# Router's end reordered on VectorE, between the router and the first expert item of a hybrid decoder trunk

## The reference

```python
def moe_swiglu(h, w_router, w1, w3, w2):
    logits = jnp.dot(xf.astype(F32), w_router.astype(F32))
    top_logit, top_e = lax.top_k(logits, TOP_K)          # 2 of 8 experts for each token
    gates = jax.nn.softmax(top_logit, axis=-1)
    ...
    padded = (counts + ROW_BLOCK - 1) // ROW_BLOCK * ROW_BLOCK
    dest = pstart[e_sorted] + (jnp.arange(n * TOP_K, dtype=jnp.int32) - start[e_sorted])
    ...
    x_rows = jnp.concatenate([xf, jnp.zeros((1, d), xf.dtype)], axis=0)[row_tok]
    def expert_block(args):
        xb, e = args
        return (jax.nn.silu(xb @ w1[e]) * (xb @ w3[e])) @ w2[e]   # 1024 -> 3584 -> 1024
    ...
    y = jax.ops.segment_sum(y_rows.astype(F32) * row_gate[:, None], row_tok, num_segments=n + 1)[:n]
```

## Time and profile before

| | before |
|---|---|
| median of 3 executions | 2046.12 us (2045.82 to 2048.55) |
| the profiled execution, whole | 2042.14 us |
| its span | 2040.5 us |
| busy PE, DVE, ACT, POOL | 98%, 77%, 54%, 6% |
| chain that ended last, by engine | PE 86%, DVE 9%, issue 2%, ACT 2% |

### The profile page before, as it was taken

How to read it: one execution, slowest core, us unless ns; L and a number is a source line. 1 busy time by engine, 2 the same in 40 slices (tenths; PEclk the granted TensorE clock), 3 DMA queues, 4 the chain that set the end, 5 groups by cost and what they waited for, 6 DMA issues and landing times.

```text
span 2040.5 us, 34437 instructions
## 1 busy us (share of the span) xinstructions
PE 1990.0 (98%) x12290; PEld 1761.5 (86%) x12291; DVE 1570.0 (77%) x1978; ACT 1101.6 (54%) x1273; POOL 116.5 (6%) x104
## 2 busy tenths in 40 slices
PE   7999999999999999999999999999999999999997
PEld 6889787878779788999999988888999888999875
DVE  6866535353557585888888899999888898888998
ACT  6532423232335423555655577777655777555775
POOL 0000000000000000300100010100100100000250
PEclk9999999999999999999999999999999999999999
DMA  5312723232322123877787799999877899877993
GB/s 198 105 61 93 269 82 103 82 103 82 106 79 83 62 73 131 247 267 260 240 279 247 248 343 379 352 390 362 282 264 258 290 384 353 280 255 247 332 410 130
DMA packets 218751, 449.50 MB, mean 220 GB/s; under 512 B 13264, under 2 KB 64480, under 8 KB 218704
## 3 DMA queue, kind: packets, MB, share of 16 engines
q1 hardware_dynamic: 210560, 421.05, 59.1%
q0 software_dynamic: 8144, 27.82, 3.6%
HBM read 431.87 MB, written 16.96 MB: 220 GB/s over the span
## 4 chain that ended last, share of the span: by engine, by line
PE 86%; DVE 9%; issue 2%; ACT 2%; DMA 0%; DVEq 0%; ACTq 0%; SPq 0%; POOLq 0%
PE ps L617 17%; PE ps L619 17%; PE ps L618 17%; PE ps L959 15%; PE ps L976 8%; PE ps L961 6%; PE ps L978 3%; DVE w_lo L1845 1%; PE ps L686 1%; DVE w_lo L1848 1%; DVE w_lo L1401 1%; PE ps L641 1%; DVE ex L1426 1%; ACT w_hi L1251 0%; PE ps L880 0%
## 5 line engine op out<-in xcount | busy, mean ns | idle before, releaser
L959 PE MATMUL ps<-xt,w_hi 128*128 128x304 f32 x1792 | 457.2, 345 | 2.9 <-issue 2.9
L1845 DVE TENSOR_TENSOR w_lo<-raw,w_hi 128x1024 fp32r<-128x1024 f32 x336 | 409.3, 1218 | 55.3 <-ACT w_hi L1251 52.2
L1251 ACT ACTIVATE w_hi<-raw 128x1024 fp32r<-128x1024 f32 x340 | 357.7, 1052 | 123.5 <-PE ps L961 73.3
L961 PE MATMUL ps<-xt,w_lo 128*128 128x152 f32 x1792 | 420.0, 234 | 0.0
L1848 DVE TENSOR_TENSOR w_lo<-raw,w_hi 128x1024 fp32r<-128x1024 f32 x336 | 408.8, 1217 | 0.0
L1253 ACT ACTIVATE w_hi<-raw 128x1024 fp32r<-128x1024 f32 x340 | 356.5, 1049 | 1.1 <-DMA raw<-in_moe_w_dram 1.1
L961 PEld LDWEIGHTS ps<-xt,w_lo 128*128 128x128 f32 x1792 | 342.9, 191 | 0.1
L959 PEld LDWEIGHTS ps<-xt,w_hi 128*128 128x128 f32 x1792 | 338.8, 189 | 3.5 <-issue 3.4
L617 PE MATMUL ps<-act_hi,w_hi 128*128 128x512 f32 x608 | 242.1, 398 | 5.2 <-DVE act_lo L1446 5.2
L619 PE MATMUL ps<-act_hi,w_lo 128*128 128x512 f32 x608 | 239.9, 395 | 0.0
L618 PE MATMUL ps<-act_lo,w_hi 128*128 128x512 f32 x608 | 239.8, 394 | 0.0
(11 more groups left out here) (362 smaller groups left out, 3222.6 us busy)
## 6 DMA issues: line engine op xcount, KB each, us to landing
raw<-in_moe_w_dram SPq DMA_DIRECT2D x672, 512.0 KB, 5.4
raw<-in_w_in_dram SPq DMA_DIRECT2D x19, 1024.0 KB, 5.1
raw<-in_ffn_w_gate_dram SPq DMA_DIRECT2D x11, 1024.0 KB, 5.3
raw<-in_ffn_w_up_dram SPq DMA_DIRECT2D x11, 1024.0 KB, 5.3
raw<-in_ffn_w_down_dram SPq DMA_DIRECT2D x11, 1024.0 KB, 4.9
raw<-in_w_out_dram SPq DMA_DIRECT2D x8, 1024.0 KB, 4.9
y_rows<-mult POOLq DMA_DIRECT2D x1, 8192.0 KB, 28.9
y_rows<-yacc POOLq DMA_DIRECT2D x7, 512.0 KB, 5.2
```

What stands on the lines that cost most here:

```text
L959: pe.matmul(pairs_of(ps[:, bank, 0:2 * NW]), hi_[:, k % 4, f * P:(f + 1) * P], xt[:, k, :, 0:NW], start=k == 0, stop=False)
L961: last = pe.matmul(ps[:, bank, NW:2 * NW], lo_[:, k % 4, f * P:(f + 1) * P], xt[:, k, 0, 0:NW], start=False, stop=k == KT - 1)
L1251: act.activation(slot_hi[p % 6][:, 0:half], raw6(p)[:, 0:half], ACT.Copy).then_inc(w_hi_half, 1)
L1845: dve.tensor_tensor(slot_lo[p % 6][:, 0:half], raw6(p)[:, 0:half], f32(slot_hi[p % 6][:, 0:half]), ALU.subtract)
```

## The change

On DVE, the low part of piece 0 is split: its first half stays ahead of the ranks, its second half moves behind the first part of the item list. The semaphore `pick_ready` is raised for each token tile, and PE waits for tile i before its first matmul that uses it. The item list is made in two parts: the number of items, the last item and the flags for the turned form come early (`items_ready` 1), the expert and block of each item late (`items_ready` 2). Between the two lie now the rest of piece 0, piece 1, the low parts of the picked rows, and pieces 2 and 3. The computation of `slots` comes behind these. SP and POOL wait for 2, PE and ACT still for 1. PE's fillings are 6 and 6 in place of 13 and 14.

```diff
             expert(0, 0, True)
-            sp.wait_ge(items_ready, 1)
+            sp.wait_ge(items_ready, 2)
...
-            pool.wait_ge(items_ready, 1)
+            pool.wait_ge(items_ready, 2)
...
-            spin(ps[:, 7, 0:P], 13)
-            pe.wait_ge(pick_ready, 1)
+            spin(ps[:, 7, 0:P], 6)
             for k in range(KT):
                 for i in range(NT):
+                    if k == 0:
+                        pe.wait_ge(pick_ready, i + 1)
                     last = pe.matmul(ps[:, k // 3, k % 3 * NW:(k % 3 + 1) * NW], rows_of(3, i)[:, k * P:(k + 1) * P],
                                      pick[:, i, :], start=i == 0, stop=i == NT - 1)
...
-            spin(ps[:, 7, 0:P], 14)
+            spin(ps[:, 7, 0:P], 6)
             turned_next = pe.alloc_register("pe_turned_next")
             pe.wait_ge(items_ready, 1)
...
+            def rest_half(p, at_, late):
+                half = PIECE // 2
+                s_ = slice(late * half, (late + 1) * half)
+                if late:
+                    dve.wait_ge(w_hi_done, MOE0 + p + 1 if at_ is None else at_ + (MOE0 + p + 1))
+                else:
+                    dve.wait_ge(w_hi_half, p + 1 if at_ is None else at_ + (p + 1))
+                ins = dve.tensor_tensor(slot_lo[p % 6][:, s_], raw6(p)[:, s_], f32(slot_hi[p % 6][:, s_]), ALU.subtract)
+                if late:
+                    ins.then_inc(w_lo_done, 1)
...
-            rest_ahead(0, None)
+            rest_half(0, None, 0)
             dve.wait_ge(rank_done, 1)
...
+            link(dve.tensor_copy(items[0:1, 48:64], flags))
+            link(dve.tensor_copy(items[0:1, 32:33], items_to[:, NE - 1:NE]))
+            dve.tensor_copy(items[0:1, 33:34], last_item[:, NE - 1:NE]).then_inc(items_ready, 1)
+            dve.wait_ge(items_ready, 1)
+
+            rest_half(0, None, 1)
+            rest_ahead(1, None)
+            picked_rows(0)
+            picked_rows(1)
+            rest_ahead(2, None)
+            rest_ahead(3, None)
...
             dve.tensor_copy(items[0:1, 0:32], rt[0:1, 18, :]).then_inc(items_ready, 1)
-            dve.wait_ge(items_ready, 1)
-            picked_rows(0)
-            picked_rows(1)
-            rest_ahead(2, None)
-            rest_ahead(3, None)
             dve.wait_ge(par_act, DEPTH + 1)
```

More of the change, by code:

```diff
@@ L1840, in _ @@
             slot_lo = [w_los[:, (MOE0 + j) % 3, :] for j in range(3)] + [w_lo2[:, j, :] for j in range(3)]
-            def rest_ahead(p, at_):
[L1843 to L1849, removed]
+            def rest_half(p, at_, late):
[8 more added lines that the diff above has]
+                    ins.then_inc(w_lo_done, 1)
+            def rest_ahead(p, at_):
+                for late in range(2):
+                    rest_half(p, at_, late)
             def picked_rows(j):
@@ L1869, in _ @@
             for i in range(NT):
-                ins = dve.tensor_scalar(pick[:, i, :], mcon[:, MC_ROW:MC_ROW + NW], rt[:, RK, i * NE:i * NE + 1],
-                                        rt[:, CH, i * NE:i * NE + 1], ALU.is_equal, ALU.mult)
-            ins.then_inc(pick_ready, 1)
+                dve.tensor_scalar(pick[:, i, :], mcon[:, MC_ROW:MC_ROW + NW], rt[:, RK, i * NE:i * NE + 1],
+                                  rt[:, CH, i * NE:i * NE + 1], ALU.is_equal, ALU.mult).then_inc(pick_ready, 1)
             link(dve.tensor_reduce(cnt, ps[:, 4, 0:NT * NE].rearrange("p (t e) -> p e t", e=NE), AX.X, ALU.add))
@@ L1877, in _ @@
             link(dve.tensor_tensor(first_block, blocks_to, blocks, ALU.subtract))
[L1879 to L1886, removed]
             w3v = [rtw[0:1, i, :].rearrange("p (n e) -> p n e", e=NE) for i in range(5)]
@@ L1902, in _ @@
             link(dve.tensor_tensor_scan(items_to, items_e, zero_row[0:1], 0.0, ALU.add, ALU.add))
+            link(dve.tensor_scalar(last_item, items_to, -1.0, None, ALU.add))
+            link(dve.tensor_tensor(w3v[3], n_row, over_n(last_item), ALU.is_equal))
+            link(dve.tensor_tensor(w3v[3], w3v[3], over_n(turned_e), ALU.mult))
+            link(dve.tensor_reduce(flags, w3v[3], AX.X, ALU.add))
+            link(dve.tensor_copy(items[0:1, 48:64], flags))
[8 more added lines that the diff above has]
+            rest_ahead(3, None)
+            link(dve.tensor_scalar(rt[:, 15, 0:8], first_block, float(P), None, ALU.mult))
+            link(dve.tensor_tensor(r3(SLOT), r3(RK), per_e(rt[:, 15, 0:8]), ALU.add))
+            for j, oh in enumerate((OH1, OH2)):
+                link(dve.tensor_tensor(r3(PROD), r3(SLOT), r3(oh), ALU.mult))
+                link(dve.tensor_reduce(rt[:, 16, 4 * j:4 * j + 4], r3(PROD), AX.X, ALU.add))
+                link(dve.tensor_copy(slots[:, :, j], rt[:, 16, 4 * j:4 * j + 4]))
+            dve.tensor_copy(tokens[:, :], mcon[:, MC_TOK:MC_TOK + NT]).then_inc(slots_ready, 1)
             link(dve.tensor_tensor(first_item, items_to, items_e, ALU.subtract))
             link(dve.tensor_tensor(shift, first_block[0:1], first_item, ALU.subtract))
-            link(dve.tensor_scalar(last_item, items_to, -1.0, None, ALU.add))
             link(dve.tensor_tensor(w3v[0], n_row, over_n(first_item), ALU.is_ge))
@@ L1913, in _ @@
             link(dve.tensor_tensor(rt[0:1, 18, 16:32], rt[0:1, 18, 16:32], n_row[:, :, 0], ALU.add))
-            link(dve.tensor_tensor(w3v[3], n_row, over_n(last_item), ALU.is_equal))
-            link(dve.tensor_tensor(w3v[3], w3v[3], over_n(turned_e), ALU.mult))
-            link(dve.tensor_reduce(flags, w3v[3], AX.X, ALU.add))
             link(dve.tensor_scalar(rt[0:1, 18, 16:32], rt[0:1, 18, 16:32], float(MAX_BLOCKS - 1), None, ALU.min))
-            link(dve.tensor_copy(items[0:1, 48:64], flags))
-            link(dve.tensor_copy(items[0:1, 32:33], items_to[:, NE - 1:NE]))
-            link(dve.tensor_copy(items[0:1, 33:34], last_item[:, NE - 1:NE]))
             dve.tensor_copy(items[0:1, 0:32], rt[0:1, 18, :]).then_inc(items_ready, 1)
-            dve.wait_ge(items_ready, 1)
-            picked_rows(0)
-            picked_rows(1)
-            rest_ahead(2, None)
-            rest_ahead(3, None)
             dve.wait_ge(par_act, DEPTH + 1)
```

## The result

| | before | changed |
|---|---|---|
| median | 2047.07 us (2044.18 to 2050.69, 22 runs) | 2053.58 us (2046.12 to 2057.42, 22 runs) |
| ratio | | 1.0026, 95% interval 1.0018 to 1.0035 |
| profiled execution, and its span | 2042.14, 2040.5 us | 2048.03, 2046.4 us |

The change made the kernel slower by 0.26%, 5.3 us, where 1.1 us was forecast; the medians lie 6.5 us apart. The 22 times of the changed kernel fall into two heaps: 5 between 2046.1 and 2048.0, 17 between 2051.4 and 2057.4.

A forecast was written before the change was run, and what follows sets the result against it. DVE, without slack, was taken to bound the kernel until hidden_turned releases PE, then PE alone. +0.8 us for DVE, +0.3 for the clock, nothing for POOL or PE's earlier start: 2046.12 + 1.1 = 2047.2 us, range 2044.0 to 2049.8.

The forecast's parts named there:

- The sign of the forecast: Whole kernel: slower by 1.1 us, to 2047.2 us; chance 0.90 of staying within 0.2% (4.1 us).
- DVE sets the down pass, PE's early start brings nothing.: Item 0: DVE's hidden_turned releases PE's down pass, so PE's 3.7 us earlier start and the dip's 1.7 go into waiting.
- +0.8 us on DVE.: Router on DVE: factors end at 834.1 instead of 833.3, through new waits of 0.2 for ranks and 0.5 for ACT.
- PE's stop of 5 to 6 us at the down pass, near 862.4.: Item 0 on PE: waits some 5 to 6 us for hidden_turned where it waited 0.38, ending at 862.4.
- +0.3 us for the clock after that stop.: PE behind the down-pass stop: lower clock costs between nothing and 0.55 us, taken as 0.3.
- POOL, nothing.: POOL's scatters and clearing of yturned: start 11.5 us later, end at 858.1, with 10.6 us of slack, no cost.
- The removed fillings, nothing but their time.: PE ahead of picks and item 0: fillings at 0.12 us each, six and six ending about 812.9 and 822.2; no other cost.
- No rival of mine: PE's earlier start counts, up to 5.4 us gained (full 0.05, partial 0.10); POOL's lateness delays DVE (over 4.1 us 0.05, smaller 0.02).

The follow-up runs named there:

- The experiment with early signals: Changed kernel with 60 early waits and DVE's signals y_added and item_out moved to just behind the picked rows' low parts; ratio 1.0007 against the kernel before.
- 30 instructions at the start: Changed kernel, fillings still 6 and 6, with 60 waits on a long-raised semaphore (30 instructions) at PE's program start; 2047.75 us, ratio 1.0000 against the kernel before.
- 60 instructions on: Kernel before with 120 waits on a long-raised semaphore at PE's program start, 60 instructions more ahead of the item loop; ratio 1.0008.

## Why the prediction was wrong

The sign of the forecast was right (+1.1 us); that it would stay within 0.2%, and below 2049.8 us, was not. Step by step:

- **DVE sets the down pass, PE's early start brings nothing.** Right for both kernels. Item 0 took 186.3 to 186.5 us in the profiles with the old order and the factors ahead, whatever PE did (six of them). With ten of DVE's instructions taken away it took 184.3, and 182.7 without the lower clock, and PE had no wait for DVE left: beyond some 2 us PE's own path counts again.
- **+0.8 us on DVE.** Nearly right. From `fold` to the `hidden_turned` that in the kernel before last releases PE, the changed order took 0.6 us more in the profile (809.55 to 868.61, against 806.15 to 864.63, both by the timeline). The two waits are there, 0.19 for the ranks and 0.36 for ACT, and they are all of it. With 71 fillings and no lower clock in it, item 0 took 0.5 us more.
- **PE's stop of 5 to 6 us at the down pass, near 862.4.** The sum of the stops was right (3.36 + 1.86), the place was not: I overlooked the wait for `item_out` ahead of the first up pass. The experiment with early signals shows that it made no difference to the time.
- **+0.3 us for the clock after that stop.** Too small for the first profile, where item 0 has 1.6 us beyond DVE's 0.5 (188.4 against 186.3). I bounded it from the one dip of 3.4 us that the profile before shows, at the start of item 0. In the new order it lasted 6.8 us in three of the profiles with the factors ahead: the first, that with early signals, and that with 6 and 21 fillings. Over the seven profiles with the new order and the factors ahead, item 0 took 186.8 to 189.1 us, 187.2 in the middle: 0.9 us more than the old order, where the sum said 1.1. So for item 0 by itself the sum came out near, in part by luck: DVE's term was too large by some 0.2 to 0.3 us, and the clock's, from nothing with 71 fillings to 2.3 with 6 and 21, depended on the execution.
- **POOL, nothing.** Right: its work ended at 862.0, and nobody waited.
- **The removed fillings, nothing but their time.** This is the step that failed. I counted them as PE's time in a slack and not as program. They are 30 instructions ahead of the item loop. With them gone, the first jump over the other form's code waits for an instruction packet in most executions of the changed kernel: 3.5 us in its profile (3.3 to 4.0 in the four profiles that have the stop), then 6.8 us at the lower clock, together about 6.3 us, in about 17 of 22 runs, if each run of the upper heap had it (one profile of each heap was taken, and they bear that out). 17/22 x 6.3 = 4.9, with item 0's 0.9 that is 5.8 us, beside the 5.3 of the ratio and the 6.5 of the medians. No rival of mine had it. Given back by any of three ways (27 fillings in the old places, 30 instructions at the start, 27 fillings in new places), the changed kernel stands at 0.9999, 1.0000 and 1.0000, where item 0's 0.9 us alone would be 1.0004; the intervals of 0.0009 either side can't tell these apart.

What stays open is why the same program meets the stop in some executions and not in others. In the first profile of the changed kernel the packet started at 1007.7 us, 3.0 ahead of the jump, while PE still turned rows. In the second one it started at 1007.2, just as PE ended its turns, which was 3.5 us earlier than in the first. The jump seems to stand near the point where the sequence ahead is asked for; this was argued, not shown. The order seems to have a share in how often it happens: the kernel before with 12 fillings has the same loop position, and only 3 of its 11 runs lie above 2051.4 us, where 17 of 22 of the changed kernel do. So it is the new order and the missing fillings together that make up the loss of 0.26%; the missing fillings alone cost 0.11% (0.01 to 0.21). And with 100 instructions more a packet came early and the stop came all the same; that the jump's target then lies one block further fits this, but no run tests it. Nor was it tried to move the block borders inside the loop without changing what stands ahead of it.

## What to carry to other kernels

An instruction taken away or added ahead of a loop moves the loop against the blocks in which the program is loaded. Look for stops of an engine with no releaser where it first jumps forward, compare them and the instruction packets around them before and after, and try another number of fillings before judging the order itself. And where an engine's wait has another engine behind it that has no slack, an earlier start is worth nothing: take work off that other engine, and look again, since soon the first engine is the limit. Ten small instructions moved to a later item, together with more fillings in a wait, gave 4.7 us (2.9 to 6.6). The fillings without the move gave none, nor did the new order with its fillings given back.

## What the runs showed of the hardware

- A jump that found its code not loaded stopped PE for 3.3 to 4.0 us (four profiles), with a packet of 16 KB starting on the instruction queue within 0.05 us of the stop's begin. In the other 13 the stop was 0.25 to 0.61 us, and a packet had started 3.0 us or more ahead. From 7 us after the jump on, no trace has another packet of PE's queue as long as the loop runs, which is six items more after item 1: the loop then stays loaded.
- After the stop between the items the granted clock was 0.50 (1.2 of 2.4 GHz) for 6.8 us in three profiles (stops of 3.5, 3.7 and 4.0 us) and for 3.4 us in the fourth (3.3 us), against the 3.4 us of the dips in the earlier trace rows. Stops of 1.85 to 1.98 us ahead of the down pass in item 0 came with 6.8 us of it in one profile, with 3.4 in three and with none in two, and the stop of 2.5 us ahead of item 0 with 3.4 us in the kernel before and with none in one of its variants (60 instructions on). So the same stop does not always bring the lower clock.
- A wait on a semaphore that is already raised is not free. PE's first work of all starts at 9.4 to 10.7 us without such waits and with 60 of them, at 12.4 and 13.8 with 120, at 15.8 with 180 and at 17.8 with 200. From 120 to 200 that is 0.05 to 0.07 us each.
